# Reordering the first projection groups of a fused two-block mixer: z by tokens first, the convolution in half steps

## The reference

```python
h = rms_norm(x, pre_norm_w)
proj = h @ w_in                      # (256, 2048) @ (2048, 12304)
gdn_qkv, gdn_z, gdn_b, gdn_a, moba_qkv, moba_z, gate_a, gate_b = split(proj)
qkv = silu(causal_depthwise_conv(gdn_qkv, conv_w))     # 4 taps, along the tokens
qa, ka, va = split(qkv)              # 8 heads of 128 each
oa = gated_delta_rule(l2_normalize(qa), l2_normalize(ka), va, beta, g)   # chunked
oa = oa * rsqrt(mean(oa * oa)) * gdn_norm_w * silu(gdn_z)
u_a = oa @ w_branch_a
u_b = (moba_attention(moba_qkv) * silu(moba_z)) @ w_branch_b
merged = sigmoid(gate_a) * u_a + sigmoid(gate_b) * u_b
x = x + rms_norm(merged @ w_out, post_norm_w)          # then the second mixer
```

## Time and profile before

| | us |
|---|---|
| median of three runs | 1226.79 (1226.12 to 1228.09) |
| the profiled execution | 1226.49 |
| its span, first to last instruction | 1224.7 |
| TensorE busy | 1205.6 |
| VectorE busy | 747.6 |
| ScalarE busy | 604.9 |
| GpSimd busy | 96.7 |

### The profile page before, as it was taken

How to read it: one execution, slowest core, us unless ns; L and a number is a source line. 1 busy time by engine, 2 the same in 40 slices (tenths; PEclk the granted TensorE clock), 3 DMA queues, 4 the chain that set the end, 5 groups by cost and what they waited for, 6 DMA issues and landing times.

```text
span 1224.7 us, 16300 instructions
## 1 busy us (share of the span) xinstructions
PE 1205.6 (98%) x6462; PEld 1003.3 (82%) x6462; DVE 747.6 (61%) x995; ACT 604.9 (49%) x893; POOL 96.7 (8%) x135
## 2 busy tenths in 40 slices
PE   9999999999999999999999999999999999999997
PEld 9888888888878888888888888788898677778886
DVE  5678875665666655556455555667466646865654
ACT  6665555544324546444434444464453455666443
POOL 0000011189200000000000000000000000000000
PEclk9999999999999999999999999999999999999999
DMA  8656664576644545655665686555644756656562
GB/s 274 206 172 173 184 196 140 151 215 192 175 140 122 180 128 140 218 182 169 216 190 188 192 300 194 183 189 175 203 127 142 237 165 192 225 153 204 190 196 98
DMA packets 141099, 224.03 MB, mean 183 GB/s; under 512 B 9968, under 2 KB 60848, under 8 KB 140000
## 3 DMA queue, kind: packets, MB, share of 16 engines
q1 hardware_dynamic: 138576, 212.30, 56.8%
q0 software_dynamic: 2128, 9.64, 2.3%
q10 hardware_dynamic: 320, 1.06, 0.2%
HBM read 218.25 MB, written 4.72 MB: 182 GB/s over the span
## 4 chain that ended last, share of the span: by engine, by line
PE 92%; DVE 2%; ACT 2%; SPq 1%; issue 1%; DMA 1%; POOL 0%; POOLq 0%; ACTq 0%; DVEq 0%
PE acc L1988 63%; PE acc L1967 11%; PE acc L1969 5%; PE aux L1859 3%; PE acc L1920 2%; PE aux L2205 1%; PE aux L2232 1%; DMA raw_w<-in_w_in 1%; DVE lo_w L1317 1%; SPq L755 1%; PE aux L2044 1%; PE aux L2095 1%; ACT hi_w L937 0%; PE aux L2198 0%; PE aux L2225 0%
## 5 line engine op out<-in xcount | busy, mean ns | idle before, releaser
L1317 DVE TENSOR_TENSOR lo_w<-raw_w,hi_w 128x1024 fp32r<-128x1024 f32 x379 | 463.8, 1233 | 345.4 <-ACT hi_w L937 344.1
L1988 PE MATMUL acc<-hi_w,h_both 128*128 128x512 f32 (+1 forms) x1632 | 519.6, 391 | 1.6 <-DVE lo_w L1317 1.3
L937 ACT ACTIVATE hi_w<-raw_w 128x1024 fp32r<-128x1024 f32 x379 | 394.4, 1056 | 256.0 <-PE acc L1988 209.2
L1988 PEld LDWEIGHTS acc<-hi_w,h_both 128*128 128x128 f32 x1632 | 304.6, 188 | 67.5 <-issue 5.6
L1988 PE MATMUL acc<-lo_w,h_both 128*128 128x512 f32 (+1 forms) x816 | 314.6, 386 | 0.0
L1967 PE MATMUL acc<-h_both,hi_w 128*128 128x512 f32 x576 | 204.5, 399 | 0.8 <-DVE lo_w L1317 0.8
L1988 PEld LDWEIGHTS acc<-lo_w,h_both 128*128 128x128 f32 x816 | 153.6, 188 | 28.2
L1969 PE MATMUL acc<-h_both,lo_w 128*128 128x256 f32 x576 | 161.1, 280 | 0.0
L1967 PEld LDWEIGHTS acc<-h_both,hi_w 128*128 128x128 f32 x576 | 108.2, 188 | 26.8 <-DVE lo_w L1317 1.2
L1969 PEld LDWEIGHTS acc<-h_both,lo_w 128*128 128x128 f32 x576 | 108.7, 189 | 0.1
L1988 PE MATMUL acc<-hi_w,m_hi 128*128 128x512 f32 x224 | 87.5, 391 | 0.0
(11 more groups left out here) (360 smaller groups left out, 1205.3 us busy)
## 6 DMA issues: line engine op xcount, KB each, us to landing
raw_w<-in_w_in SPq DMA_DIRECT2D x283, 512.0 KB, 3.8
raw_w<-in_w_out SPq DMA_DIRECT2D x64, 512.0 KB, 4.8
raw_w<-in_w_branch_a SPq DMA_DIRECT2D x16, 512.0 KB, 4.8
raw_w<-in_w_branch_b SPq DMA_DIRECT2D x16, 512.0 KB, 4.8
raw_w<-in_cmp_k_w SPq DMA_DIRECT2D x8, 512.0 KB, 4.3
raw_w<-in_cmp_v_w SPq DMA_DIRECT2D x8, 512.0 KB, 4.7
x_in<-in_x SPq DMA_DIRECT2D x8, 256.0 KB, 7.1
x<-in_x POOLq DMA_DIRECT2D x1, 2048.0 KB, 10.9
```

The source lines that it names most:

```text
L937: act.activation(hi_w[slot][:, 0:n], raw_w[no % RAW_SLOTS][:, 0:n], ACT.Copy).then_inc(*hi_ready.event(no))
L1317: dve.tensor_tensor(lo_w[slot][:, 0:n], raw_w[no % RAW_SLOTS][:, 0:n], hi_w[slot][:, 0:n].bitcast(F32), ALU.subtract).then_inc(*lo_ready.e ...
L1988: i = pe.matmul(to[:, t, 0:group.cols], x[at], w[:, k], start=first and k == 0 and m == 0, stop=last and k == n - 1 and m == 2)
```

## The change

- Group 0 is now z, heads 0 to 3, by tokens (ticks 0 to 7, and `first_products` for the first piece); q0 follows as pairs in ticks 8 to 15, and k0, v0, q1, k1, v1 each eight ticks later than before (v1 ends with tick 55). z1 keeps ticks 56 to 63. The channels form is gone.
- `r1_row` moves from tick 9 to tick 10.
- The convolution goes by halves of two channel blocks: as soon as a half (`s`) of a group is out of PSUM, its taps run, in two steps of two and one taps. The copy out of PSUM waits for the same half of the part before, not for the whole of it.
- `token_out` comes three ticks after `conv_back` in place of one, v1 excepted, and `k_scale` behind it.
- `base` is 62 in place of 55, and all steps that hang on it move by seven ticks; the first unit of the attention moves from tick 129 to 133.
- `z_out(0)` is at tick 11 and its gain at 13; `z_out(1)` stays at tick 64, its gain is at 65. `mz_out(0)` (tick 120) has a new wait, for the last `join_t` on TensorE (tick 118). The buffer `sq` moves to another place.

```diff
-    out.append(Group(("conv", "q", 0), "w_in", 0, "h1", kind="channels"))
+    out.append(Group(("z", 0), "w_in", z, "h1"))
     for h in range(2):
         for n, part in enumerate("qkv"):
-            if (part, h) != ("q", 0):
-                pairs(("conv", part, h), n * GDN_W + h * COLS)
-    for h in range(2):
-        out.append(Group(("z", h), "w_in", z + h * COLS, "h1"))
+            pairs(("conv", part, h), n * GDN_W + h * COLS)
+    out.append(Group(("z", 1), "w_in", z + COLS, "h1"))
...
-    at(9, "r1_row")
+    at(10, "r1_row")
...
+            for s in range(2):
+                c = END[("conv", part, h, s)]
+                at(c + 1, "raw_out", part, h, s)
+                for n in range(2):
+                    at(c + 2 + n, "conv", part, h, s, n)
             at(c + 4, "conv_silu", part, h)
-            if (part, h) == ("q", 0):
-                c += 1
             at(c + 5, "conv_back", part, h)
-            at(c + 6, "token_out", part, h)
-
-    base = conv_end("v", 1) + 8
+            at(c + (6 if (part, h) == ("v", 1) else 8), "token_out", part, h)
+            if part == "k":
+                at(c + 9, "k_scale", h)
+
+    base = END[("conv", "v", 1, 1)] + 7
...
-    for h in range(2):
-        at(END[("z", h)] + 1, "z_out", h)
+    at(11, "z_out", 0)
+    at(13, "z_gain", 0)
+    at(END[("z", 1)] + 1, "z_out", 1)
+    at(END[("z", 1)] + 2, "z_gain", 1)
...
-                if s == 0:
-                    act.wait_ge(*dve_did.after("conv", *before_conv(part, h)))
-                    act.wait_ge(*act_did.after("tap", *before_conv(part, h)))
+                if (part, h) == ("q", 0):
+                    act.wait_ge(*pe_did.after("x_flip", KT - 1))
+                else:
+                    act.wait_ge(*dve_did.after("conv", *before_conv(part, h), s))
+                    act.wait_ge(*act_did.after("tap", *before_conv(part, h), s))
...
-            def conv(part, h, n):
+            def conv(part, h, s, n):
...
-                for back in range(1, CONV):
-                    for i in range(2 * n, 2 * n + 2):
+                for back in ((1, 2), (3,))[n]:
+                    for i in range(2 * s, 2 * s + 2):
...
             def z_out(h):
...
-                if h == 0:
-                    act.wait_ge(*dve_did.after("ssq", "k", 1))
+                act.wait_ge(*pool_did.after("r1"))
...
             def mz_out(h):
...
+                if h == 0:
+                    act.wait_ge(*pe_did.after("join_t", 1, NT - 1))
...
-                    for c in range(QUAD):
-                        if k == 0 and c == 2:
+                    for t in range(NT):
+                        if k == 0 and t == 1:
                             x_flip(1)
-                        for m, (w, x) in enumerate(((hi, h_hi), (hi, h_lo), (lo, h_hi))):
-                            i = pe.matmul(channels_of(0)[:, c], w[:, k, c * P:(c + 1) * P], x[:, k],
-                                          start=c % 2 == 0 and k == 0 and m == 0, stop=False)
+                        at = (slice(None), k, slice(t * P, (t + 1) * P))
+                        for m, (x, w) in enumerate(((h_hi, hi), (h_hi, lo), (h_lo, hi))):
+                            i = pe.matmul(acc[:, 0, t], x[at], w[:, k], start=k == 0 and m == 0, stop=False)
```

More of the change, by code:

```diff
@@ L638, in acc_of @@
             return acc[:, PIECES[tick][0] % 2]
-        def channels_of(tick):
-            return acc_of(tick).rearrange("p b (i c) -> p (b i) c", c=SEQ)
         def pairs_of(tick):
@@ L1019, in m_out @@
                     *act_did.event("half", "moba", part, h, s))
-            def conv(part, h, n):
+            def conv(part, h, s, n):
                 if n:
                     return
-                act.wait_ge(*dve_did.after("raw_out", part, h))
+                act.wait_ge(*dve_did.after("raw_out", part, h, s))
                 if (part, h) != ("q", 0):
@@ L1027, in conv @@
                 first = "qkv".index(part) * HEADS + h * QUAD
-                for i in range(QUAD):
+                for i in range(2 * s, 2 * s + 2):
                     tap = act.activation(cv[:, i], raw[:, i], ACT.Copy,
                                          scale=conv_w[:, CONV - 1, first + i:first + i + 1])
-                tap.then_inc(*act_did.event("tap", part, h))
+                tap.then_inc(*act_did.event("tap", part, h, s))
             def conv_silu(part, h):
-                act.wait_ge(*dve_did.after("conv", part, h))
+                for s in range(2):
+                    act.wait_ge(*dve_did.after("conv", part, h, s))
                 if (part, h) == ("v", 1):
@@ L1406, in raw_out @@
             def raw_out(part, h, s):
[L1408 to L1416, removed]
                 to = raw[:, 2 * s:2 * s + 2]
                 sum_pairs(to, ("conv", part, h, s), ("raw_sum", part, h, s))
-                key = ("raw_out", part, h) if s else ("raw_half", part, h)
-                dve.tensor_tensor(to, to, over_heads(r1_row[:], 2), ALU.mult).then_inc(*dve_did.event(*key))
+                dve.tensor_tensor(to, to, over_heads(r1_row[:], 2), ALU.mult).then_inc(
+                    *dve_did.event("raw_out", part, h, s))
             def m_out(part, h, s):
@@ L1426, in m_out, with conv @@
                 dve.tensor_tensor(to, to, over_heads(r1_row[:], 2), ALU.mult).then_inc(*dve_did.event(*key))
-            def conv(part, h, n):
-                dve.wait_ge(*act_did.after("tap", part, h))
+            def conv(part, h, s, n):
+                dve.wait_ge(*act_did.after("tap", part, h, s))
                 first = "qkv".index(part) * HEADS + h * QUAD
-                for back in range(1, CONV):
-                    for i in range(2 * n, 2 * n + 2):
+                for back in ((1, 2), (3,))[n]:
+                    for i in range(2 * s, 2 * s + 2):
                         last = dve.scalar_tensor_tensor(
@@ L1439, in conv @@
                 if n:
-                    last.then_inc(*dve_did.event("conv", part, h))
-                else:
-                    link(last)
+                    last.then_inc(*dve_did.event("conv", part, h, s))
             def token_out(part, h):
@@ L1554, in delta_norm, with z_gain @@
                 last.then_inc(*flip_source.event("oa", h))
-            def z_out(h):
+            def z_gain(h):
                 dve.wait_ge(*act_did.after("z", h))
@@ L1835, in _ @@
                      "join_y": join_y, "join_t": join_t,
-                     "delta": delta, "delta_norm": delta_norm, "z_out": z_out, "att": att, "flip": flip,
+                     "delta": delta, "delta_norm": delta_norm, "z_gain": z_gain, "att": att, "flip": flip,
                      "branch": branch, "y_out": y_out, "y_last": y_last, "y_rest": y_rest, "residual": residual, "h2_lo": h2_lo, "split": split,
@@ L1970, in products @@
                                           stop=last and k == n - 1)
-                    i.then_inc(*used.event(no))
-                    return
-                if group.kind == "channels":
-                    for c in range(group.cols // P):
-                        for k in range(n):
-                            for m, (w, x) in enumerate(((hi, x_hi), (hi, x_lo), (lo, x_hi))):
-                                i = pe.matmul(channels_of(no)[:, c], w[:, k, c * P:(c + 1) * P], x[:, k0 + k],
-                                              start=first and c % 2 == 0 and k == 0 and m == 0,
-                                              stop=last and c % 2 == 1 and k == n - 1 and m == 2)
                     i.then_inc(*used.event(no))
```

17 lines of the change are left out of this document (1 added, 16 removed).

## The result

The changed kernel took 1228.76 us, the median of 20 executions (1227.19 to 1233.12). The kernel before, on the same chips, took 1227.32 (20 executions, 1226.12 to 1228.20). The ratio is 1.0014, with an interval of 1.0008 to 1.0020: slower by 1.4 us, inside the bound of 0.2%. Its profiled execution took 1228.6 us, with a span of 1226.8 against 1224.7.

A forecast was written before the change was run, and what follows sets the result against it. TensorE, busy 98% of the span, was taken as the bound. Gains of 1.7 and 1.0, against losses of 0.4, 2.45 and 1.2 less 0.27, gave +1.1, trimmed to +0.8: 1227.6 us, range 1224.2 to 1229.9.

The forecast's parts named there:

- part 4: Middle of the kernel: eight token pieces leave and eight pairs come, 2.77 us a piece against 2.72, a loss of 0.4.
- Part 1: First eight pieces by tokens: 2.80 us each, 0.16 less than now, 1.1 us gained over P1 to P7.
- Part 2: Row of norms after P10: P10 starts at 39.95 after waiting 0.8; 1.7 us gained together with the token pieces.
- Part 3: Convolution in smaller steps: the wait at P15 goes because k's copy no longer waits for all of q; 1.0 us gained.
- rival C: The wait at P15 only moves, as z's silu at tick 11 takes ScalarE's slack: +1.8, 1228.6 us; chance 0.08.
- the last "few tenths": A small wait of a step of v0 removed, and roundings of the queues, bring the summed +1.1 us to +0.8.
- Part 5: Chains seven ticks later meet z1's silu and the attention's copies: first chain +2.45 us, second +1.2, third -0.27, fourth covered.
- Rival A: The chains are not held by z1's silu, so the kernel is faster: about -2.7, 1224.1 us; chance 0.13.
- B: Copies of queries or keys share the decay's tick and hold three of four chains: +3.2, 1230.0 us; chance 0.12.
- Rival D: Each ScalarE table switch costs twice its load, 1.38 us more on the first and second chains: +3.6, 1230.4; chance 0.03.
- The solve on GpSimd, its way back and the chunks' state keep their distances in ticks, so I take 0: Later steps behind the chains: moved along by the same ticks, they add no time.
- The attention's 0: Attention's first four units, four ticks later with one more pair of table loads: between -0.4 and +1.3 us, taken as 0.

The follow-up runs named there:

- the three edits of the old order: On the kernel before: row of norms in tick 10, 1228.81 us; copy of k0's first half one tick later, 1226.23; both, 1225.64.

## Why the prediction was right, and where it was not

The forecast was 1227.6 us, 0.8 over the median shown before; measured were 1.4 us of difference between medians and 2.1 between spans. "Within 0.2%" was the likeliest case, for the reason given: about 2.7 us won before P16, and more than that lost where z1's silu meets the decay. That the total is as close as it is has some luck in it: 1.1 us of gain ahead of the chains (part 4) and 1.7 of waits behind them (1.28 at the solve, and 0.23, 0.16 and 0.30 less 0.24 after it) were both unforeseen, and mostly cancel. Some 0.8 of the distance at 794.79 was not located. The steps in their order:

- **Part 1, pieces by tokens: the size was off.** P1 to the transposes behind it is 2.85 us (12.11 to 14.96), and P2 the same (15.32 to 18.17). A token piece costs 2.85, not the 2.80 I put together from a stretch of three (which is 8.27 and not 8.23 long: 187.52 to 195.56, and 0.227), and saves 0.11, not 0.16. P8 came at 34.23, not 33.5: 0.4 won in place of 1.1; P1's later start, which is this execution's, is 0.3 of the difference, seven times 0.05 the rest.
- **Part 2: right, and it hid that error.** P10 starts when its low half is there, not when TensorE is free: 40.06, forecast 39.95. Its wait is 0.19 (last start ahead of it 39.75, room after 0.12), not 0.8. A term that ends in a wait for another engine is safe from errors in the terms ahead of it.
- **Part 3: right.** P15 doesn't wait, P16 starts at 57.28, forecast 57.3; rival C, by which the wait only moves to z's early silu, falls (P12 doesn't wait; silu's table is loaded at 41.61 while TensorE works). What I had not seen, and the three edits of the old order show, is that parts 2 and 3 are not a sum.
- **Part 4 and the last "few tenths": wrong in sign.** Forecast from P16 to the chains was a loss of 0.4 less 0.3, and no row stood behind the 0.3. Measured against the old order with its chains in the same ticks, the lead grows there by 1.0 (2.9 to 3.9). A wait of 0.17 ahead of v0's transposes (103.50 to 103.79 before) is the small wait that was meant. Another 0.4 is that eight ticks of pairs take 22.70 us (104.61 to 127.31) in the kernel before and 22.27 or 22.28 in all such stretches of the changed one. The rest is open.
- **Part 5, the chains: right in mechanism and size.** Forecast 0.41 + 2.45 = 2.86 for the first. By the same reckoning, from starts, it is 2.69 (last start 211.94, room at 212.06, start 214.75; the profile shows 2.54). For the second 1.2 was forecast, and it is 1.15 (228.95, 229.07, 230.22; shown as 0.98). For the third and fourth no wait was forecast, and there is none. z_out(1) ahead of the decay takes both away (-4.5), and the chains alone bring the loss into the old order (+6.1, of which the fall of the clock is 2.7). Rival A, no chain held, falls. So does B, by which the queries' copies hold three chains: the third and fourth are in time at 244.58 and 258.93.
- **Rival D, a table switch that costs twice, falls.** Silu's load starts at 206.88, its first activation at 208.17, 1.29 later, and the first wait is shorter than forecast, not longer. The Trainium skill (ScalarE: Activation LUTs, What ACT_TABLE_LOAD costs) has a drain of 1380 ns beside the load; no row here shows it.
- **"The solve on GpSimd, its way back and the chunks' state keep their distances in ticks, so I take 0": this step failed.** Distances in ticks hold for what runs at TensorE's pace; a way through DRAM does not. From the load to the first step back it took 73.8 us where it had taken 68.0, and cost 1.28 and 1.71 in two profiles and nothing in others. The row that I had was one sample, with no wait at `lift` and no sign of how far it was from one. The chunks' state did not keep its margins either: waits of 0.23 and 0.30 come with the seven ticks, in the old order too.
- **The attention's 0 held.** There is one pair of table loads more (440.30 to 503.30), no wait of TensorE goes with it, and the wait of 0.24 for `att_o` at 487.42 is gone.
- **No term for the clock.** I priced waits by their length. Of two executions with the same wait of 2.54, one paid another 1.3 us; the range held that, the sum did not. The kernel before has executions with a low mean clock as well, so both medians contain some of it.

## What to carry to other kernels

Where two steps share a tick, write out the queue of each engine in the order of issue: whether an activation with another table stands ahead of a step that waits anyway, or behind it and ahead of the split on which the matmuls hang, was worth 4.5 us here with the same work in the same tick. When a step at TensorE's start is made earlier, find the next result that doesn't come earlier with it, and change both together or neither. And give every trip through DRAM a margin of its own, in microseconds and not in ticks, since one profile shows only one sample of its length.

## What the runs showed of the hardware

A wait on TensorE can cost its length and then some. Behind waits of 2.54 us (the kernel with the later `lift`), 2.91 (the chains seven ticks later) and 2.95 (the row of norms alone) the granted clock was 0.50, the 1.2 GHz level, with pairs 0.64 us apart in place of 0.35. By the means of single microseconds it began to fall before the wait's end in the first two (0.71 from 214 to 215, 0.63 from 218 to 219) and 1 to 2 us behind it in the third (1.00 from 58 to 59, 0.64 from 59 to 60), and was full again at 218, 226 and 63 us. They cost 1.3, 2.7 and some 1.8 us more than the wait. Behind waits of 1.71 us and less it stayed in these profiles. Behind the wait of 2.54 in the profiled execution of the changed kernel it stayed as well, so that the length alone does not decide. A third of the executions of the kernel before (27 of 82) have a mean clock as low as these, though the longest wait of its profile is 1.19 us; why is open. Matmuls of no use in the wait (0.66 idle left of it) kept the clock up and took 1.7 us off the median of the kernel with the later `lift`.

The Trainium skill (TensorE: Matmul & The Clock Gate, HAM oscillation) says that a wait between two stretches of TensorE's work lets the clock drop again; the trace agrees, with 2.54 to 2.95 us of idleness, and adds that the same wait may also pass without it.

The load of the blocks through GpSimd's queue took 3.9 us from start to landing in one place of the plan and 5.4 to 7.2 one tick earlier, with the same bytes, and the same solve on GpSimd took 60.1 to 62.4 us over the 14 profiles. What sets either was not tried.
